# Differential attention on one core: exponentials in their own step, an earlier difference of maps, a gate load on ScalarE's queue

## The chip, the cores and the metric

One core of a Trainium2 chip runs the whole program. The metric is the device time of one execution in microseconds. The engines are TensorE (PE; PEld is its weight load), VectorE (DVE), ScalarE (ACT), GpSimd (POOL) and the queues that issue DMAs, here SyncE's (SPq) and ScalarE's (ACTq).

## The reference

Two layers of a hybrid decoder. Each layer norms its input, projects it to 4224 columns, runs an RWKV-7 branch and a differential attention branch, gates both with SiLU and projects the result back. The prompt has 2048 tokens; 8 decoded sequences of 4 tokens use a paged cache of 2048 past tokens each (16 pages of 128). The change is in the attention alone:

```python
def diff_attend(q, k, v, q_pos, k_pos, lam):
    s = jnp.einsum('bqhcd,bkhcd->bhcqk', q, k) / math.sqrt(DIFF_HEAD_DIM)
    s = jnp.where(k_pos[None, :] <= q_pos[:, None], s, -jnp.inf)
    p = jax.nn.softmax(s, axis=-1)
    attn = p[:, :, 0] - lam * p[:, :, 1]
    return jnp.einsum('bhqk,bkhe->bqhe', attn, v)
...
    o = attend(q, k, v, lam)
    o = rms_norm(o, subln_w, SUBLN_EPS) * (1.0 - lam_init)
    diff_out = o.reshape(B, T, DIFF_WIDTH) * jax.nn.silu(diff_gate.astype(f32))
```

There are 4 heads; each has two maps (c = 0, 1) over 64 dimensions and values of 128.

## The kernel before

A loop over the 2 layers runs five phases, each closed by a barrier: projection, RWKV prompt, attention, RWKV of the decoded sequences, output projection. Every engine has its own program; semaphores order them. Attention is written out flat, with no loop in hardware.

The prompt's attention goes by row tiles of 128 queries: tile t of 64 is head t // 16, step s = t % 16 of that head. `ORDER` alternates short and long rows (0, 15, 1, 14, ...), so that even s have short rows (128 to 1024 keys) and odd s long ones (2048 down to 1152). A row is cut in blocks of 512 keys: `blocks(t)` is 1 or 2 in even steps and 4 or 3 in odd ones. Work on tile t is spread over three steps:

- step t: TensorE makes the scores of both maps per block (`scores`, L1352, and the mask on the last block, L1357) into one of two pairs of PSUM banks; VectorE evicts them to S0 and S1 (`scores_out`, L1259) and then takes the maximum (`maxima`, L1264, L1265), which releases `mx_ok`.
- step t + 1: ScalarE takes the exponentials in place, S0 at j = 0 and S1 at j = 1 (`exp`, L1163), which release `ex_ok`; at the end of the step VectorE forms S0 = S0 + c S1 (`combine`, L1270 to L1272), which releases `cb_ok`.
- step t + 2: TensorE turns the map by blocks through one bank (`turn_map`, L1368), ScalarE copies it out (`copy_turned`, L1172), TensorE multiplies it with the values (`values`, L1380); at the end ScalarE copies the output and its squares (`copy_o`, L1177, L1178), which releases `o_ok`, for which the next tile's values wait.

Step t has `width(t)` = max(blocks(t), blocks(t-2) + 2) places j. From j = 1 on each holds some work beside (`beside`): turning the head's values (L1390, copied at L1210; s = 2 and 3), turning the finished output of the head before (L1397, used at L1295; s = 5 and 7), or the next piece of a decoded sequence: turning a page of keys (L1123, copied by ScalarE at L1039), scores against four pages (L1115, evicted at L1078), the exponentials of all its scores (L1047, L1049, L1050), turning them (L1127, L1132, copied at L1053, L1060), and the products with pages of values (L1143). In each head one sequence has its exponentials around s = 7 and the other one at s = 14. At j ScalarE does the copy of the page that TensorE turns at j + 1.

Once per head VectorE forms sums (`head_sums`, s = 1, L1276 to L1280, needs the last output copy), ScalarE takes their root (`head_root`, s = 4, L1182, with a switch of tables) and VectorE scales the output (`head_scaled`, s = 4, L1287). The gate of the head lies in `cg`: loaded by SP (L1013), its tanh at s = 12 to 15 (L1189), gated at L1291, the head's result formed in place (L1295) and stored by ScalarE's queue at s = 8 of the next head (L1193). The load of the next gate waits for that store.

SP's queue holds the pages of keys (L970; 4 buffers, each waits for its turning) and of values (L979; two groups of 4 pages), the maps' queries and keys (L988), the values (L1008) and the gate, in one order.

Of the kernel before, what the change touches and what calls it, by code (L numbers as in the profile page):

```python
# [45 lines left out]
Q_ROW, K_ROW, V_ROW, DG_ROW = 2176, 2688, 3200, 3712  # L46
# [68 lines left out]
def build(nc, ins, outs):  # L115
# [4 lines left out]
    with ctx:  # L120
# [756 lines left out]
        cg = cv(SEQ)  # L877
# [27 lines left out]
        c_v, c_g, c_lam, c_lv, mask_ok = [csem(n) for n in ("in_v", "in_gate", "lam", "lv", "mask")]  # L905
        c_kq, c_cst, u_in, c_sto = [sem(n) for n in ("c_in_kq", "c_cst", "u_in", "c_store")]
# [74 lines left out]
        def map_rows(l, h, r):  # L981
            return PT[bass.ds(l * COLS + h * P + r, P), 1:SEQ + 1]
# [21 lines left out]
        def attn_sync(sp, l):  # L1004
            def load_values(h):
                if h:
                    t_full(sp, "v", h - 1, 3)
                sp.dma_start(vT[:, :], map_rows(l, h, V_ROW)).then_inc(c_v, 16)  # L1008

            def load_gate(h):  # L1010
                if h:
                    sp.wait_ge(c_sto, 16 * h)
                sp.dma_start(cg[:, :], map_rows(l, h, DG_ROW)).then_inc(c_g, 16)  # L1013
            load_values(0)
            sp.wait_ge(u_in, U_IN)
            keys_sync(sp, l, 0, range(KS))
            for b in range(NSEQ):
                h = b // 2
                keys_sync(sp, l, b, range(KS, 8))
                values_sync(sp, l, b, (0, 1))  # L1020
                if b % 2 and h + 1 < HEADS:
                    load_maps(sp, l, h + 1)
                keys_sync(sp, l, b, range(8, NP))
                if b % 2 and h + 1 < HEADS:
                    load_values(h + 1)
                if b + 1 < NSEQ:
                    keys_sync(sp, l, b + 1, range(KS))
                values_sync(sp, l, b, (2, 3))
                if b % 2 == 0:
                    load_gate(h)  # L1030

        def beside_scalar(act, b, k):
            if K_AT <= k < K_AT + NP:
# [118 lines left out]
        def attn_scalar(act, l):  # L1152
            act.wait_ge(c_lam, 1)
            act.activation(lamv[:, 2:4], lamv[:, 0:2], ACT.Exp).then_inc(c_lam, 1)
            act.wait_ge(u_in, U_IN)
            act.activation(sg_s[:, :, :], g_s[:, :, :], ACT.Tanh, scale=0.5).then_inc(so_rt, 1)

            def exp(t, a):
                i, w = row(t), (row(t) + 1) * P
                if a == 0:  # L1160
                    act.wait_ge(mx_ok, t + 1)
                src = S1[:, t % 2, 0:w] if a else S0[:, t % 3, 0:w]
                e = act.activation(src, src, ACT.Exp, bias=nm[:, t % 2, a:a + 1], accum_out=l12[:, par(t), i, a:a + 1])  # L1163
                if a:
                    e.then_inc(ex_ok, 1)

            def copy_turned(t, j):
                G, w = first(t) + j, min(4, row(t) + 1 - 4 * j)
                act.wait_ge(pt_ok, G + 1)
                if G >= 4:  # L1170
                    act.wait_ge(v_ok, G - 3)
                act.activation(PT_[:, G % 4, 0:w, :], bank[4][:, 0:w * P].rearrange("p (c t) -> p c t", t=P), ACT.Copy).then_inc(pa_ok, 1)  # L1172

            def copy_o(t):
                i = row(t)
                act.wait_ge(v_ok, first(t) + blocks(t))
                act.activation(O[:, par(t), i, :], bank[5][:, 0:P], ACT.Copy)  # L1177
                act.activation(osq[:, :], bank[5][:, 0:P], ACT.Square, accum_out=ssq[:, par(t), i:i + 1]).then_inc(o_ok, 1)  # L1178

            def head_root(h):  # L1180
                act.wait_ge(fs_ok, h + 1)
                act.activation(fs[:, :], fs[:, :], ACT.Sqrt).then_inc(rt_ok, 1)  # L1182

            def gate_tanh(h, g):
                if g == 0:
                    act.wait_ge(c_g, 16 * (h + 1))
                if 4 * h + g >= 2:
                    act.wait_ge(sg_ok, 4 * h + g - 1)
                act.activation(tg[:, g % 2, :], cg[:, g * GRP:(g + 1) * GRP], ACT.Tanh, scale=0.5).then_inc(gt_ok, 1)  # L1189

            def store_head(h):
                act.wait_ge(oe_ok, 4 * h + 4)
                act.dma_start(MT[bass.ds(RW + h * P, P), 0:SEQ], cg[:, :]).then_inc(c_sto, 16)  # L1193
            for t in range(NTILE + 2):
                h, s_ = t // NT, t % NT
                if h and s_ == 8 and t < NTILE:
                    store_head(h - 1)
                for j in range(width(t)):
                    if j < 2 and 1 <= t <= NTILE:
                        exp(t - 1, j)  # L1200
                    if j < blocks(t - 2):
                        copy_turned(t - 2, j)
                    if j == 0 and h and s_ == 4:
                        head_root(h - 1)
                    if j == 0 and 12 <= s_:
                        gate_tanh(h, s_ - 12)
                    if (t, j + 1) in V_AT:
                        vh, vg = V_AT[t, j + 1]
                        t_full(act, "v", vh, vg)
                        act.activation(vtok[:, 4 * vg:4 * vg + 4, :], TB.rearrange("p (c t) -> p c t", c=4), ACT.Copy).then_inc(t_out, 1)  # L1210
                    for b, k in pieces(t, j + 1):
                        beside_scalar(act, b, k)
                if t >= 2:
                    copy_o(t - 2)
            head_root(HEADS - 1)
            act.wait_ge(so_sum, 1)
            act.activation(ors[:, :, :], SB[:, 0:P].rearrange("p (c t) -> p c t", c=4), ACT.Sqrt, bias=lamv[:, 6:7], scale=1.0 / P).then_inc(so_rt, 1)
            store_head(HEADS - 1)
            act.wait_ge(u_lv, 7)
            act.dma_start(MT[RW:D, SEQ:TOK].rearrange("(h p) t -> p h t", p=P), omx[:, :, :]).then_inc(u_sto, 16)  # L1220
            act.wait_ge(u_sto, 16)

        def attn_vector(dve, l):
# [82 lines left out]
            for t in range(NTILE + 2):  # L1306
                h, s_ = t // NT, t % NT
                for j in range(blocks(t)):
                    scores_out(t, j)
                    beside(t, j)  # L1310
                if t < NTILE:
                    maxima(t)
                if 1 <= t <= NTILE:
                    combine(t - 1)
                if 12 <= s_ < 16:
                    gate(h, s_ - 12)
                for j in range(blocks(t), width(t)):
                    beside(t, j)
                if h and s_ == 1:
                    head_sums(h - 1)  # L1320
                if h and s_ == 4:
                    head_scaled(h - 1)
# [763 lines left out]
```

## Time and profile before

| | us |
|---|---|
| median of 3 runs | 4914.3 (4902.1 to 4914.8) |
| profiled execution | 4913.2 |
| its span | 4911.4 |
| TensorE busy | 4096.3 (83%) |
| VectorE busy | 2023.2 (41%) |
| ScalarE busy | 1751.4 (36%) |
| chain that ended last | TensorE 67%, VectorE 12%, ScalarE 8% |
| attention, layer 0 | 1495 to 2177 |
| attention, layer 1 | 3891 to 4578 |

Busy time is that in which an engine executes; TensorE's busy time depends on its granted clock, shown as a share of full speed. A row of the timeline gives start, duration, engine, line, operation, output and inputs with shapes, the number of merged instructions, and in brackets the idle time before it with what ended it. Microseconds are counted from the start of the span. A row of the stretches gives its bounds and length, the busy time and number of instructions of each engine, the mean granted clock, the share of the DMA engines and their rate.

### The profile page before, as it was taken

What the parts mean: (1) busy time and instruction counts of PE and PEld (TensorE: products, weight loads), DVE (VectorE), ACT (ScalarE), POOL (GpSimd) and SP (SyncE); (2) the same over time, 40 slices, a digit from 0 to 9 for tenths busy, and PEclk for the clock granted to TensorE, in tenths of its full rate; (3) what the DMA queues carried; (4) which work ended last, traced back from release to release, by engine and by line L of the source; (5) the groups of instructions that cost most, each with busy time, mean ns of one, the idle gap of its engine ahead of it and who ended that gap; (6) DMA issues with size and microseconds to landing.
All of it is one profiled execution on the core that took longest, in us unless ns stands there. A gap on an engine that the chain in (4) does not pass through costs nothing.

```text
span 4911.4 us, 114297 instructions
## 1 busy us (share of the span) xinstructions
PE 4096.3 (83%) x49138; PEld 3564.4 (73%) x49138; DVE 2023.2 (41%) x4536; ACT 1751.4 (36%) x3584; POOL 481.6 (10%) x264
## 2 busy tenths in 40 slices
PE   3999998788887887877979999978888788788595
PEld 2999998677774555556979999967777555555495
DVE  3111111666655555552231111136666455555335
ACT  3000000666655555651110000036666555565211
POOL 1322231000000000001033222200000000000200
PEclk9999999799998999987989999979999899999697
DMA  4211121111113344343222111111111244353333
GB/s 162 78 70 74 65 77 61 39 44 37 39 45 113 127 147 133 100 146 121 84 75 76 68 74 70 57 63 38 39 44 28 80 143 122 118 164 97 115 120 131
DMA packets 227651, 427.63 MB, mean 87 GB/s; under 512 B 32162, under 2 KB 137636, under 8 KB 212900
## 3 DMA queue, kind: packets, MB, share of 16 engines
q1 hardware_dynamic: 213316, 339.18, 21.7%
q10 hardware_dynamic: 13824, 81.07, 4.1%
q8 instruction: 390, 6.39, 0.5%
q14 instruction: 121, 0.99, 0.1%
HBM read 304.91 MB, written 123.80 MB: 87 GB/s over the span
## 4 chain that ended last, share of the span: by engine, by line
PE 67%; DVE 12%; ACT 8%; issue 5%; SPq 4%; DMA 4%; POOL 1%; ACTq 0%; DVEq 0%
PE psum L1881 10%; PE psum L1882 10%; PE psum L1883 10%; PE psum L1352 4%; PE psum L1380 3%; PE psum L703 3%; PE psum L1526 3%; PE psum L1528 2%; PE psum L1527 2%; PE psum L1368 2%; PE psum L1123 2%; SPq L978 2%; PE psum L700 2%; SPq L979 2%; PE psum L774 1%
## 5 line engine op out<-in xcount | busy, mean ns | idle before, releaser
L1881 PE MATMUL psum<-x_hi,w_parts 128*128 128x416 f32 x2640 | 931.4, 353 | 60.5 <-POOL w_parts L1839 60.5
L1882 PE MATMUL psum<-x_lo,w_parts 128*128 128x416 f32 x2640 | 927.3, 351 | 0.0
L1883 PE MATMUL psum<-x_hi,w_parts 128*128 128x416 f32 x2640 | 926.7, 351 | 0.0
L1848 DVE TENSOR_TENSOR arena<-psum,arena 128x416 f32<-128x416 f32 x330 | 195.5, 592 | 1284.5 <-PE psum L1883 1284.3
L322 ACT ACTIVATE arena<-arena 128x256 f32<-128x256 f32 x16 | 8.2, 514 | 1543.9 <-DVE arena L446 1543.9
L1881 PEld LDWEIGHTS psum<-x_hi,w_parts 128*128 128x128 f32 x2640 | 496.8, 188 | 68.7 <-POOL w_parts L1839 64.2
L1259 DVE TENSOR_SCALAR_CACHE_REDUCE arena<-psum 128x512 f32<-128x512 f32 (+3 forms) x640 | 357.5, 607 | 358.6 <-PE psum L1352 221.9
L1883 PEld LDWEIGHTS psum<-x_hi,w_parts 128*128 128x128 f32 x2640 | 497.1, 188 | 6.5
L1882 PEld LDWEIGHTS psum<-x_lo,w_parts 128*128 128x128 f32 x2640 | 498.2, 189 | 4.4
L1380 PE MATMUL psum<-arena 128*128 128x128 f32 x2176 | 316.9, 288 | 64.0 <-ACT arena L1172 46.8
L1352 PE MATMUL psum<-arena 64*128 64x512 f32 (+3 forms) x1280 | 325.8, 613 | 40.8 <-DVE arena L1259 22.0
L1380 PEld LDWEIGHTS psum<-arena 128*128 128x128 f32 x2176 | 284.1, 202 | 78.3 <-issue 51.4
L1163 ACT ACTIVATE arena<-arena 128x128 f32<-128x128 f32 (+15 forms) x256 | 309.0, 1207 | 8.2 <-DVE arena L1265 8.2
L1705 POOL MEMSET arena<- 128x32 f32 x2 | 0.3, 156 | 2684.0 <-SPq L107 2684.0
L1526 PE MATMUL psum<-m_hi,wo_hi 128*128 128x416 f32 x640 | 229.4, 358 | 39.6 <-DVE m_lo L1497 39.6
L1172 ACT ACTIVATE arena<-psum 128x512 f32<-128x512 f32 (+3 forms) x320 | 170.3, 532 | 248.8 <-PE psum L1368 248.7
L1836 POOL TENSOR_TENSOR w_parts<-arena 128x1024 fp32r<-128x1024 f32 (+1 forms) x68 | 129.0, 1896 | 1305.6 <-PE psum L1883 978.8
L1039 ACT ACTIVATE arena<-psum 128x512 f32<-128x512 f32 x256 | 154.9, 605 | 261.7 <-PE psum L1123 261.6
L1368 PE MATMUL psum<-ident,arena 128*128 128x128 f32 x1088 | 189.6, 292 | 67.7 <-DVE arena L1272 43.7
L1368 PEld LDWEIGHTS psum<-ident,arena 128*128 128x128 f32 x1088 | 124.0, 147 | 162.0 <-DVE arena L1272 68.5
L1528 PE MATMUL psum<-m_hi,wo_lo 128*128 128x416 f32 x640 | 226.5, 354 | 0.0
L703 PE MATMUL psum<-arena 64*64 64x64 f32 x5120 | 196.3, 229 | 35.7 <-DVE arena L508 27.2
(339 smaller groups left out, 6783.8 us busy)
## 6 DMA issues: line engine op xcount, KB each, us to landing
out_proj_t<-arena ACTq DMA_DIRECT2D x66, 1040.5 KB, 4.2
arena<-in_cache_k SPq DMA_DIRECT2D x256, 256.0 KB, 2.8
arena<-in_cache_v SPq DMA_DIRECT2D x256, 256.0 KB, 3.0
arena<-in_w_in SPq DMA_DIRECT2D x66, 512.0 KB, 3.5
arena<-out_proj_t SPq DMA_DIRECT2D x32, 1024.0 KB, 6.7
arena<-out_proj_t SPq DMA_DIRECT2D x96, 257.0 KB, 3.2
m_raw<-mixed_t SPq DMA_DIRECT2D x10, 1664.0 KB, 7.2
x_res<-x_cur SPq DMA_DIRECT2D x10, 1664.0 KB, 18.1
```

The lines of the kernel that those rows point to most:

```text
L703: mm = pe.matmul(b8(2)[at(h, j), ix(c, h), :], Yp[at(h, j), ix(c, h), :], XT[at(h, j), u % 2, ix(c, h), :], start=True, stop=True)
L1163: e = act.activation(src, src, ACT.Exp, bias=nm[:, t % 2, a:a + 1], accum_out=l12[:, par(t), i, a:a + 1])
L1259: x_ = dve.tensor_scalar(dst, bank[2 * (J % 2) + a][:, 0:w], 0.125, NEG, ALU.mult, ALU.max, accum_out=mxp[:, t % 2, a, j:j + 1])
L1352: mm = pe.matmul(bank[2 * (J % 2) + a][:, 0:w], kq[h % 2][hs(a), 0, i * P:(i + 1) * P], kq[h % 2][hs(a), 1, j * GRP:j * GRP + w], start=Tr ...
L1368: mm = pe.transpose(bank[4][:, c * P:(c + 1) * P], S0[:, t % 3, k * P:(k + 1) * P], ident[:, :])
L1380: mm = pe.matmul(bank[5][:, 0:P], PT_[:, G % 4, c, :], vtok[:, k, :], start=(k == 0), stop=(k == i))
L1526: pe.matmul(bank[q % 3][:, 0:TG], wh, mh, start=(k == 0), stop=False)
L1528: mm = pe.matmul(bank[q % 3][:, 0:TG], wl, mh, start=False, stop=(k == KT - 1))
L1848: dve.tensor_tensor(ost[:, b % 2, 1 + g * TG:1 + (g + 1) * TG], bank[q % 8][:, 0:TG], RSTD[:, cols(g)], ALU.mult).then_inc(p_ev, 1)
L1881: pe.matmul(bank[q % 8][:, 0:TG], w_hi[:, b % 3, k, :], x_hi[:, k, cols(g)], start=(k == 0), stop=False)
L1882: pe.matmul(bank[q % 8][:, 0:TG], w_hi[:, b % 3, k, :], x_lo[:, k, cols(g)], start=False, stop=False)
L1883: mm = pe.matmul(bank[q % 8][:, 0:TG], w_lo[:, b % 3, k, :], x_hi[:, k, cols(g)], start=False, stop=(k == KT - 1))
```

## The change

Three edits in the attention phase. The two exponentials of tile t move from step t + 1 (j = 0 and 1, ahead of the copy of a turned map) to the end of step t: in most steps both stand at the last place, behind the page copy there and ahead of `copy_o`. The difference of tile t - 1 moves on VectorE from behind the maximum of step t to behind the first eviction of step t. The gate's load moves from SP's queue, behind the value pages of every second sequence, to ScalarE's queue ahead of s = 10, with the same wait for the store.

```diff
@@ attn_sync
-            def load_gate(h):
-                if h:
-                    sp.wait_ge(c_sto, 16 * h)
-                sp.dma_start(cg[:, :], map_rows(l, h, DG_ROW)).then_inc(c_g, 16)
...
-                if b % 2 == 0:
-                    load_gate(h)
@@ attn_scalar
+            def load_gate(h):
+                if h:
+                    act.wait_ge(c_sto, 16 * h)
+                act.dma_start(cg[:, :], map_rows(l, h, DG_ROW)).then_inc(c_g, 16)
...
+                if s_ == 10 and t < NTILE:
+                    load_gate(h)
                 for j in range(width(t)):
-                    if j < 2 and 1 <= t <= NTILE:
-                        exp(t - 1, j)
                     if j < blocks(t - 2):
                         copy_turned(t - 2, j)
...
                     for b, k in pieces(t, j + 1):
                         beside_scalar(act, b, k)
+                    for a in range(2):
+                        if t < NTILE and j == min(blocks(t) + 1 + a, width(t) - 1):
+                            exp(t, a)
                 if t >= 2:
                     copy_o(t - 2)
@@ attn_vector
                 for j in range(blocks(t)):
                     scores_out(t, j)
+                    if j == 0 and t:
+                        combine(t - 1)
                     beside(t, j)
                 if t < NTILE:
                     maxima(t)
-                if 1 <= t <= NTILE:
+                if t == NTILE:
                     combine(t - 1)
```

## Rows read from the trace of the kernel before

**Rows 1.** Attention stretches: busy PE, PEld, DVE, ACT, POOL; clock, DMA share, GB/s.

```profile
1495.00:2177.00 682.00, 563.04 (x4595) 383.62 (x4596) 370.46 (x1156) 399.78 (x888) 0.00 (x0) 0.92 0.41 129
3891.00:4578.00 687.00, 562.48 (x4606) 385.23 (x4606) 374.72 (x1162) 399.93 (x888) 0.00 (x0) 0.92 0.41 128
```

**Rows 2.** Waits of TensorE in 1495 to 2177: total us, times, longest.

```profile
PE psum L1123 <- DMA arena<-in_cache_k: 25.1, 6, 8.4
PE psum L1380 <- ACT arena L1172: 23.4, 24, 1.9
PE psum L1368 <- DVE arena L1272: 21.0, 12, 3.4
PE psum L1368 <- ACT arena L1172: 12.0, 13, 2.4
PE psum L1352 <- DVE arena L1259: 11.1, 10, 2.3
```

**Rows 3.** Timeline of steps 6 and 7 of head 1: start, duration, and in brackets the wait.

```profile
1722.32 1.80 ACT L1163 ACTIVATE arena<-arena 128x1792 f32<-128x1792 f32 x1
...
1724.74 0.91 PE L1380 MATMUL psum<-arena 128*128 128x128 f32 x6 [1.31 <-ACT arena L1172]
...
1726.88 0.16 DVE L1270 RECIPROCAL arena<-arena 128x1 f32<-128x1 f32 x1 [2.36 <-ACT arena L1163]
...
1729.53 0.66 PE L1368 MATMUL psum<-ident,arena 128*128 128x128 f32 x4 [1.53 <-DVE arena L1272]
...
1731.36 1.66 PE L1352 MATMUL psum<-arena 64*128 64x512 f32 x4 [0.74 <-DVE arena L1259]
```

**Rows 4.** Timeline of steps 4 and 5 of head 1.

```profile
1696.53 1.28 ACT L1182 ACT_TABLE_LOAD   x1
1697.82 0.22 ACT L1182 ACTIVATE arena<-arena 128x16 f32<-128x16 f32 x1
...
1704.64 1.11 PE L1368 MATMUL psum<-ident,arena 128*128 128x128 f32 x4 [3.43 <-DVE arena L1272]
...
1709.17 2.08 PE L1352 MATMUL psum<-arena 64*128 64x512 f32 x4 [1.91 <-DVE arena L1259]
```

**Rows 5.** Timeline of steps 14 and 15 of head 0.

```profile
1639.48 0.69 DVE L1078 TENSOR_SCALAR_CACHE_REDUCE arena<-psum 128x512 f32<-128x512 f32 x1
...
1641.15 1.14 ACT L1047 ACTIVATE arena<-arena 128x1024 f32<-128x1024 f32 x1
...
1641.42 1.55 DVE L1272 SCALAR_TENSOR_TENSOR arena<-arena 128x1280 f32<-128x1280 f32 x1
...
1645.91 0.66 PE L1368 MATMUL psum<-ident,arena 128*128 128x128 f32 x4
```

**Rows 6.** Timeline, TensorE's waits for copies: head 1 s 2, 8, head 0 s 12.

```profile
1676.90 0.47 PE L1380 MATMUL psum<-arena 128*128 128x128 f32 x2 [2.42 <-ACT arena L1210]
...
1744.48 1.13 PE L1380 MATMUL psum<-arena 128*128 128x128 f32 x8 [1.87 <-ACT arena L1172]
...
1624.38 0.71 PE L1380 MATMUL psum<-arena 128*128 128x128 f32 x4 [0.86 <-ACT arena L1172]
```

**Rows 7.** Timelines of SP's queue and of TensorE around step 11 of head 1.

```profile
1757.35 0.33 SPq L1013 DMA_DIRECT2D arena<-out_proj_t  x1
...
1777.08 11.13 SPq L970 DMA_DIRECT2D arena<-in_cache_k  x5
...
1786.01 1.12 PE L1123 MATMUL psum<-ident,arena 128*128 128x128 f32 x4 [8.32 <-DMA arena<-in_cache_k]
```

**Rows 8.** Busy times by stretch, columns as in rows 1.

```profile
1744.00:1750.00 6.00, 5.52 (x52) 3.88 (x52) 2.93 (x7) 4.33 (x11) 0.00 (x0) 0.72 0.01 3
1704.00:1715.00 11.00, 8.06 (x30) 5.42 (x32) 8.39 (x22) 1.79 (x4) 0.00 (x0) 0.53 0.00 0
1768.00:1776.00 8.00, 7.89 (x60) 5.41 (x61) 6.86 (x21) 5.77 (x15) 0.00 (x0) 1.00 0.78 238
1778.00:1786.00 8.00, 0.00 (x0) 0.00 (x0) 0.45 (x2) 0.00 (x0) 0.00 (x0) 0.60 0.92 349
```

## The prediction

> **What bounds the kernel now.** I read the stage table first: the change touches only attention, which runs twice, and in each of the two stretches TensorE is busy 563 us of 682 and of 687 at a mean granted clock of 0.92, while VectorE and ScalarE are busy 370 to 400 us [rows 1]. So TensorE sets the time and 120 us per layer are its idle time; the change can only act on that idle time, and on the clock. The waits of TensorE by releaser come next [rows 2]: in the first layer 25.1 us for a page of keys, 23.4 and 12.0 us for the copy of a turned map (L1172), 21.0 us for the difference of maps (L1272), 11.1 us for an eviction of scores (L1259). The last two are what an earlier difference could take away: 32 us per layer, 64 us in all, is the ceiling. The second layer repeats the first [rows 1], so I work out one and double it.
>
> I name steps within a head s = 0 to 15. Odd steps hold long rows (16 down to 9 blocks of 128 keys), even ones short rows. The timeline of s = 6 and 7 shows the pattern [rows 3]: in s = 6 ScalarE does the first exponential of the long row at 1722.32 (1.80 us), copies a turned map and a page, then does the second; TensorE waits 1.31 us for that copy, VectorE 2.36 us for the second exponential, and TensorE in s = 7 another 1.53 us for the difference and 0.74 us for an eviction queued behind it. So one chain ends last: long exponentials, difference, turning.
>
> **The exponentials, step by step.** Both now stand at the end of their own step, behind the last page copy, so on ScalarE they are back to back; what is queued behind them is the output copy (L1177, L1178), the copy of the next turned map and the next page copy, for which TensorE waits. The first exponential starts only 0.4 us sooner, since the page copy before it is itself paced by TensorE. The order is bought by moving one exponential E in front of the copies.
> - s = 6 and 7: exponentials 1721.9 to 1725.5, output copy and map copy 0.9, so TensorE resumes near 1726.5 instead of 1724.74: +1.75. The difference runs 1726.0 to 1728.5, TensorE reaches the turning at 1729.8 and finds it done: 1.53 gone. The eviction behind it ends at 1730.8, and the scores that began at 1731.36 begin at 1730.9: net -0.5 [rows 3]. All four heads: -2.0 per layer.
> - s = 4 and 5, heads 1 to 3: the square root of a head lies between the two exponentials and switches tables and back, 1.28 us each time (one of the two loads is shown); TensorE then waits 3.43 us for the difference and 1.91 us for an eviction [rows 4]. After the change both exponentials come before the switch: they end at 1697.7 instead of 1701.8, the difference ends at 1700.5, the four scalings behind it at 1704.3, the next eviction at 1705.6, where the scores of 1709.17 can start: -3.5 each, -10.5 per layer. Head 0 has no square root there: +1.9 for E, -2.2 of its waits: -0.3.
> - s = 2 and 3: E is 2.0 (2048 elements, by 1.80 for 1792). The sums of a head on VectorE need the output copy, which now stands behind both exponentials, so VectorE is held until 1678 and the difference ends at 1682.2; scores that began at 1683.10 begin near 1683.9. The wait of 2.42 grows to 4.3, those in s = 3 shrink [rows 6]. +0.8 in heads 1 to 3, +1.0 in head 0: +3.4.
> - s = 8 and 9: E = 1.7 with next to nothing behind it to win back (0 to 0.2): the wait of 1.87 [rows 6] grows to 3.3: +1.4, +5.6 per layer.
> - s = 12 and 13: here TensorE does two blocks of scores before it needs a copy. The pair ends at 1620.4, just when the map is turned, and the second copy no longer stands behind an exponential: the wait of 0.86 [rows 6] goes: -3.4 per layer.
> - s = 10 and 11: +0.9 on TensorE, but in heads 0 to 2 it then waits 8.3 us for a page whose loading is timed by SP's queue [rows 7], which swallows it; head 3 pays. With +1.1 in the last two steps: +2.0 per layer.
>
> **The difference behind the first eviction.** In odd steps it is the short row's and costs nothing: VectorE idles there 2 to 3 us later in the step. In even steps it stands in front of a second eviction, the maximum, and the page work. That hurts at s = 14. There VectorE evicts page scores at 1639.48, on which the page's own exponentials wait (start 1641.15); the difference took 1.55 us plus 0.5 for its two small parts, after them [rows 5]. Moved ahead it pushes the page exponentials to 1642.7. They last 2.6 us (two of 1024 elements at 1.14, and a short one), now followed by both exponentials of a row of 1024 (2.3 us by the same 1.14), the output copy and only then the map copy: done near 1648.4. TensorE, which turned the next map at 1645.91, first waits 1.3 us for the page exponentials and then for that copy: 1648.5 to 1648.7, +2.8 in every head, +11.2 per layer. This is the largest new wait. At s = 0 a similar +1.1 falls into a wait for a page of values that is there already, nothing.
>
> **The gate.** SP's gate issue at 1757.35 leaves its queue, 0.55 us with its register work, between page loads; its wait for the store had long been met (store at s = 8). On ScalarE it is issued at the start of s = 10, near 1767, and takes 0.4 us of its sequencer, beside running activations: 0, at most 0.4 x 8 = 3 us. Its 1 MB now moves beside eight value pages (0.78 of the engines' time, 238 GB/s) and before the two maps and the key page issued at 1777.08, for which TensorE waits until 1786.01; there 349 GB/s flow [rows 7, 8]. If it fits into the spare room, that wait shrinks by 0.55; if it all lands in front, it grows by 1 MB / 349 GB/s = 3.0. I take 0, since s = 10 starts 10 us before that key page is issued.
> The Trainium skill (DMA: Bandwidth & Descriptors, Issuing engines are not separate DMA queues) says that DMAs of any issuing engine run on the same 16 DMA engines and interleave, and that another issuer saves only sequencer time. By that rule the move is worth the 0.55 us at most, and the 3.0 us are a risk; no row of before shows two issuers at once at this place.
>
> **The clock.** Stretches with long waits fall towards the level of 1.2 GHz: 0.53 in 1704 to 1715, 0.60 in 1778 to 1786. Behind the 1.87 us at s = 8 the six microseconds from 1744 had a mean of 0.72: 0.28 x 6 = 1.7 us lost [rows 8]. I charge one such loss more at s = 8 and one at s = 14, 4 x 2 x 1.7 = +13.6 per layer, and give back two thirds of the 0.47 x 11 = 5.2 us in s = 5, 3 x 3.4 = -10: +3.6 per layer.
>
> **Sum.** Per layer -2.0 - 10.5 - 0.3 + 3.4 + 5.6 - 3.4 + 2.0 + 11.2 + 0 = +6.0, with the clock +9.6; two layers +19. The profiled execution took 4913.2 us (span 4911.4), 1.1 below the median 4914.3, so 4932.
> The Trainium skill (ScalarE: Activation LUTs, What ACT_TABLE_LOAD costs) puts a switch at 1283 ns plus a drain of about 1380 ns. The load is that long here, but the square root starts 1.29 us after its load, so the trace shows no drain; by the page, s = 4 would win another 1.38 us for each of the two loads, 16 us over six heads, and the sum would be 4916.
>
> **Rivals.**
> - The early difference pays (4884). The new waits at s = 14, 8 and 2 come out at half (-20 over both layers against my sum) because TensorE has other work there, and the clock terms of +7 turn into -20. For it: 64 us of TensorE's idle time end on VectorE [rows 2]. Against: TensorE's stream is in order and the copies gate it.
> - The new waits throttle (4965). Slower than my forecast: the waits of 3 to 4 us at s = 2, 6, 8 and 14 each bring twice the loss of [rows 8]; it decides from two such waits per head on: 32 places, about 1 us each, +33.
> - The gate load collides (4950): +3.0 in six heads, +18.
> - Waits only change places (4913): what the difference gives, the copies take.
>
> **Chances.** Forecast 0.45 (its own range 4918 to 4950), early difference pays 0.22, throttling 0.13, gate 0.07, no change 0.13. Range 4886 to 4962. A measurement here can tell about 0.3% (15 us), so 4899.6 to 4929.1 is the same: faster 0.20, same 0.28, slower 0.52.
>
> **What would show it.** TensorE's wait for L1272 should fall from 21.0 to under 5 us per layer, that for L1172 rise from 23.4 + 12.0 to over 50, a wait of L1127 for the page exponentials appear, VectorE's wait before L1270 fall at s = 4. I am wrong if the copies' wait stays, or the wait at s = 14 does not appear.

## The result, and the profile after

The kernel with the change takes 4936.7 us (median of 7 runs, 4927.3 to 4944.7) where the one before takes 4912.4 (7 runs on the same chip, 4901.6 to 4914.8): a ratio of 1.0060 [1.0047, 1.0073]: 24.3 us slower by the medians, 29 by the ratio. 4932 was forecast. The profiled execution took 4942.1 us; its page begins:

```profile
span 4940.3 us, 114299 instructions
...
PE 4125.5 (84%) x49138; PEld 3586.3 (73%) x49138; DVE 2019.0 (41%) x4536; ACT 1759.7 (36%) x3584; POOL 481.9 (10%) x264
...
q1 hardware_dynamic: 212164, 330.79, 21.2%
q10 hardware_dynamic: 14976, 89.46, 4.5%
```

The gate's 8.4 MB now go by q10, ScalarE's queue. Only attention grew: from its first to its last TensorE instruction it takes 699.2 and 699.7 us in the two layers, 14.8 more in each. The stretches after the change, columns as in rows 1 (bounds and length, busy PE, PEld, DVE, ACT, POOL, granted clock, DMA share, GB/s):

```profile
1494.00:2194.00 700.00, 581.05 (x4606) 395.39 (x4606) 370.47 (x1160) 404.17 (x888) 0.00 (x0) 0.89 0.40 125
3904.00:4604.00 700.00, 573.23 (x4606) 392.59 (x4606) 370.79 (x1160) 403.71 (x888) 0.00 (x0) 0.90 0.40 125
```

Against [rows 1] this holds a surprise. TensorE's idle time is 700.00 - 581.05 = 119.0 us and 126.8, where it was 119.0 and 124.5. What grew is its busy time, by 15.7 and 10.7 us for the same work, at a clock of 0.89 and 0.90 instead of 0.92. For the first layer of the kernel before, the growth is counted from a row that holds the whole phase: the first stretch of [rows 1] ends at 2177, while the last 11 of the 4606 matmuls run until 2179.4.

```profile
1495.00:2180.00 685.00, 565.44 (x4606) 385.78 (x4606) 373.46 (x1161) 399.78 (x888) 0.00 (x0) 0.92 0.41 128
```

In sum the waits have been exchanged for others, and the same matmuls took longer at a lower clock. Where each of the two happened is worked out by steps further down.

TensorE's waits in 1492 to 2188 (total us, times, longest), to be held against [rows 2]:

```profile
PE psum L1384 <- ACT arena L1166: 35.5, 12, 3.5
PE psum L1372 <- ACT arena L1166: 31.9, 20, 3.6
PE psum L1384 <- ACT arena L1209: 18.0, 4, 4.8
PE psum L1117 <- DMA arena<-in_cache_k: 12.2, 3, 5.1
...
PE psum L1117 <- ACT arena L1033: 7.2, 14, 1.3
PE psum L1121 <- ACT arena L1044: 6.4, 4, 1.6
...
PE psum L1356 <- DVE arena L1261: 1.5, 1, 1.5
```

Lines have moved: L1356 is the scores, L1261 the eviction, L1274 the difference, L1372 the turning, L1166 its copy, L1384 the values, L1209 the copy of the head's turned values, L1117 and L1033 page and copy, L1121 the turning that waits for the page's exponentials (L1044), L1072 the eviction of page scores. The wait for the difference, 21.0 us, is gone from the list, the eviction's fell from 11.1 to 1.5, that for a page of keys from 25.1 to 12.2. In their place, the copy of a turned map rose from 23.4 + 12.0 to 67.4, and a wait of 4 x 1.6 for the page's exponentials is new.

Steps 14 and 15 of head 0, the timeline that answers to [rows 5]:

```profile
1640.58 1.55 DVE L1274 SCALAR_TENSOR_TENSOR arena<-arena 128x1280 f32<-128x1280 f32 x1
...
1643.26 0.69 DVE L1072 TENSOR_SCALAR_CACHE_REDUCE arena<-psum 128x512 f32<-128x512 f32 x1
...
1644.38 1.15 ACT L1041 ACTIVATE arena<-arena 128x1024 f32<-128x1024 f32 x1 [2.41 <-DVE arena L1078]
...
1647.11 0.29 PE L1121 MATMUL psum<-ident,arena 128*32 128x128 f32 x1 [1.60 <-ACT arena L1044]
...
1648.09 1.13 ACT L1157 ACTIVATE arena<-arena 128x1024 f32<-128x1024 f32 x1
...
1649.63 0.58 ACT L1166 ACTIVATE arena<-psum 128x512 f32<-128x512 f32 x1
...
1650.26 1.12 PE L1372 MATMUL psum<-ident,arena 128*128 128x128 f32 x4 [1.80 <-ACT arena L1166]
```

The difference runs ahead of the page's eviction, ScalarE stands idle for 2.41 us, the page's exponentials start late, and both exponentials of the next row follow them before the map is copied: the chain as forecast. TensorE waits twice. Its last row above lasts 1.12 us where the same four matmuls took 0.66 in [rows 5]. The stretch with the two waits and the one behind it:

```profile
1644.85:1650.26 5.41, 2.02 (x17) 1.32 (x15) 2.41 (x8) 5.41 (x15) 0.00 (x0) 0.88 0.00 0
1650.26:1654.00 3.74, 3.74 (x20) 3.41 (x24) 3.64 (x15) 1.71 (x5) 0.00 (x0) 0.50 0.00 0
```

TensorE was busy 2.02 of 5.41 us, and then ran 3.74 us at 0.50 (1.2 GHz): half of them, 1.9 us, are lost, as much as a wait costs. Before the change the clock stood at 1.00 in this place:

```profile
1646.00:1650.00 4.00, 4.00 (x58) 3.63 (x59) 2.89 (x15) 3.46 (x8) 0.00 (x0) 1.00 0.02 4
```

Steps 4 and 5 of head 1, which answer to [rows 4]:

```profile
1706.91 1.28 ACT L1176 ACT_TABLE_LOAD   x1
1708.21 0.21 ACT L1176 ACTIVATE arena<-arena 128x16 f32<-128x16 f32 x1
...
1710.80 1.28 ACT L1157 ACT_TABLE_LOAD   x1
```

Both exponentials of the long row ended at 1706.2, ahead of the first load, and VectorE's wait for them in front of the difference is 2.16 us where it was 5.91. No row of TensorE's timeline between 1710.08 and 1724.34 has a wait; before, it stood 3.43 and 1.91 us there. So a gain at s = 4 and 5 stands against losses at s = 14 and 15, and the experiments take them apart.

### The profile page after: what moved, and what is told of

Read it like the earlier page. It is cut to its first block, busy times and chain, and to the rows that moved or that the text cites. A ratio compares the mean times of both kernels' runs of the same rounds, so it can differ in the third digit from the quotient of the medians.

```text
span 4940.3 us, 114299 instructions
## 1 busy us (share of the span) xinstructions
PE 4125.5 (84%) x49138; PEld 3586.3 (73%) x49138; DVE 2019.0 (41%) x4536; ACT 1759.7 (36%) x3584; POOL 481.9 (10%) x264
## 4 chain that ended last, share of the span: by engine, by line
PE 70%; DVE 10%; ACT 9%; issue 4%; DMA 3%; SPq 2%; POOL 1%; ACTq 0%; DVEq 0%
PE psum L1885 10%; PE psum L1886 10%; PE psum L1887 10%; PE psum L1356 5%; PE psum L1384 4%; PE psum L703 3%; ACT arena L1157 3%; PE psum L1530 3%; PE psum L1532 2%; PE psum L1531 2%; PE psum L1117 2%; PE psum L1372 2%; PE psum L700 2%; PE psum L774 1%; PE psum L1137 1%
## 5 line engine op out<-in xcount | busy, mean ns | idle before, releaser
L1261 DVE TENSOR_SCALAR_CACHE_REDUCE arena<-psum 128x512 f32<-128x512 f32 (+3 forms) x640 | 362.3, 607 | 410.8 <-PE psum L1356 283.5
L1384 PE MATMUL psum<-arena 128*128 128x128 f32 x2176 | 322.1, 293 | 107.0 <-ACT arena L1166 70.9
L1384 PEld LDWEIGHTS psum<-arena 128*128 128x128 f32 x2176 | 290.7, 206 | 116.2 <-ACT arena L1172 103.7
L1356 PE MATMUL psum<-arena 64*128 64x512 f32 (+3 forms) x1280 | 342.4, 641 | 21.8 <-SPq L107 18.7
L1033 ACT ACTIVATE arena<-psum 128x512 f32<-128x512 f32 x256 | 154.5, 604 | 273.5 <-PE psum L1117 273.3
L1372 PE MATMUL psum<-ident,arena 128*128 128x128 f32 x1088 | 186.9, 289 | 64.1 <-ACT arena L1166 64.1
L1372 PEld LDWEIGHTS psum<-ident,arena 128*128 128x128 f32 x1088 | 122.2, 146 | 160.7 <-ACT arena L1166 93.8
L1166 ACT ACTIVATE arena<-psum 128x512 f32<-128x512 f32 (+3 forms) x320 | 170.5, 533 | 187.5 <-PE psum L1372 186.3
L1531 PE MATMUL psum<-m_lo,wo_hi 128*128 128x416 f32 x640 | 225.6, 352 | 0.0
```

Source lines behind the costliest of these rows:

```text
L1261: x_ = dve.tensor_scalar(dst, bank[2 * (J % 2) + a][:, 0:w], 0.125, NEG, ALU.mult, ALU.max, accum_out=mxp[:, t % 2, a, j:j + 1])
L1356: mm = pe.matmul(bank[2 * (J % 2) + a][:, 0:w], kq[h % 2][hs(a), 0, i * P:(i + 1) * P], kq[h % 2][hs(a), 1, j * GRP:j * GRP + w], start=Tr ...
L1372: mm = pe.transpose(bank[4][:, c * P:(c + 1) * P], S0[:, t % 3, k * P:(k + 1) * P], ident[:, :])
L1384: mm = pe.matmul(bank[5][:, 0:P], PT_[:, G % 4, c, :], vtok[:, k, :], start=(k == 0), stop=(k == i))
L1531: pe.matmul(bank[q % 3][:, 0:TG], wh, ml, start=False, stop=False)
```

## The experiments

Theory A, the forecast's: three separate things. The exponentials' move takes the root and its table loads out of the chain to the difference (gain) and delays the copies (loss); the difference's move delays the page's exponentials at s = 14 (loss); the gate's does nothing. Rival B: the early difference pays and the exponentials' delays make the loss. Rival C: the gate's load collides. The ratios are against runs of the kernel before on the same chip, whose medians were 4908.2 us (for the single edits and the late difference at s = 14), 4905.9 (for the two moves of the root and the two edits on top of them) and 4908.6 (for the other three).

**The three edits one at a time.** First the exponentials alone, on the kernel before:

```diff
                 for j in range(width(t)):
-                    if j < 2 and 1 <= t <= NTILE:
-                        exp(t - 1, j)
...
                         beside_scalar(act, b, k)
+                    for a in range(2):
+                        if t < NTILE and j == min(blocks(t) + 1 + a, width(t) - 1):
+                            exp(t, a)
```

> The kernel before with the two exponentials of a tile in its own step and nothing else; the difference stays at the end of VectorE's step, the gate on SP's queue. My theory (the exponentials ahead of the copies cost about one exponential per even step and give back the waits for the difference in s = 5 and 7; the early difference adds only the delay at s = 14): the wait of TensorE for the page exponentials at s = 15 (1.6 us in the changed kernel) is gone, s = 14 and 15 together cost about 2 us over before instead of 4.1, s = 4 and 5 win 5 us in heads 1 to 3, and the time is 8 to 16 us below the changed kernel, +8 to +16 us over before: about 4923. Rival 1 (the early difference is what takes away the waits for the difference): the waits for L1272 stay near 21 us per layer and the time is at or above that of the changed kernel, 4937 or more. Rival 2 (the exponentials alone are the loss and the difference costs nothing): 4937.

Measured: 4914.9 us, 1.0004 [0.9993, 1.0015]. No change that can be told: below the 4923 that was expected and the 4937 of both rivals. The wait for the difference, 21.0 us in twelve places, has fallen to a single one of 1.3 us, at the first tile, without any move of the difference. TensorE's waits of that kernel in the first layer:

```profile
PE psum L1381 <- ACT arena L1172: 35.5, 12, 3.5
PE psum L1369 <- ACT arena L1172: 28.7, 20, 3.6
PE psum L1123 <- DMA arena<-in_cache_k: 22.6, 4, 7.3
...
PE psum L1353 <- DVE arena L1260: 3.2, 5, 1.5
```

Then the difference alone:

```diff
                     scores_out(t, j)
+                    if j == 0 and t:
+                        combine(t - 1)
                     beside(t, j)
                 if t < NTILE:
                     maxima(t)
-                if 1 <= t <= NTILE:
+                if t == NTILE:
                     combine(t - 1)
```

> The kernel before with the difference behind the first eviction and nothing else. VectorE then waits for the second exponential, which is still behind a map copy and a page copy in the next step, in front of the second eviction and the page scores. My theory: at s = 14 the page exponentials start about 3 us later (8 places, +21 us in all), at s = 12 the second eviction comes 1 us too late (+7), the even steps with one block put the maximum behind the difference: +20 to +35 us, about 4940. Rival (VectorE has slack, so the place of the difference is free): 4912, no change.

Measured: 4978.7 us, 1.0128 [1.0106, 1.0150], 63 to 70 us slower by ratio and medians, about twice the upper end of what was expected. VectorE's own waits for the second exponential say why. The kernel before (total us, times, longest):

```profile
DVE arena L1270 <- ACT arena L1163: 89.2, 32, 6.2
```

The kernel after:

```profile
DVE arena L1272 <- ACT arena L1157: 62.0, 32, 8.6
```

The difference alone:

```profile
DVE arena L1270 <- ACT arena L1163: 169.5, 60, 6.3
```

With the exponentials at j = 0 and 1, the second is not done when the first eviction is, and VectorE stands in front of the second eviction. VectorE's timeline of this kernel at step 14 of head 1:

```profile
1822.10 0.17 DVE L1270 RECIPROCAL arena<-arena 128x1 f32<-128x1 f32 x1 [2.57 <-ACT arena L1163]
...
1822.61 1.55 DVE L1272 SCALAR_TENSOR_TENSOR arena<-arena 128x1280 f32<-128x1280 f32 x1
...
1825.30 0.69 DVE L1078 TENSOR_SCALAR_CACHE_REDUCE arena<-psum 128x512 f32<-128x512 f32 x1
```

ScalarE's at the same place:

```profile
1826.41 1.15 ACT L1047 ACTIVATE arena<-arena 128x1024 f32<-128x1024 f32 x1 [3.96 <-DVE arena L1084]
```

ScalarE waits 3.96 us for VectorE in turn. So the two edits are not a sum: alone +2 and +63 to +70, together +24. The own-step exponentials are what makes the early difference bearable. Rival B falls with these two runs: the difference alone does not pay, and the exponentials alone make no loss.

The gate alone:

```diff
-                sp.dma_start(cg[:, :], map_rows(l, h, DG_ROW)).then_inc(c_g, 16)
...
+                act.dma_start(cg[:, :], map_rows(l, h, DG_ROW)).then_inc(c_g, 16)
...
+                if s_ == 10 and t < NTILE:
+                    load_gate(h)
```

> The kernel before with the gate's load on ScalarE's queue ahead of s = 10 and nothing else. My theory: no change, between -5 and +5 us; the page wait at s = 11 moves by less than 1 us. Rival (the 1 MB lands in front of the maps and the key page): that wait grows by up to 3.0 us in six heads, +18 us, 4930.

Measured: 4903.4 us, 0.9985 [0.9971, 0.9998]: at most a small gain, and no loss. Rival C falls.

**The suspected place alone.** The kernel after, with the difference late at s = 14 and nowhere else:

```diff
-                    if j == 0 and t:
+                    if j == 0 and t and s_ != 14:
                         combine(t - 1)
...
-                if t == NTILE:
+                if t == NTILE or s_ == 14:
                     combine(t - 1)
```

> The changed kernel with the difference back behind the maximum at s = 14 alone (4 tiles per layer), early everywhere else. My theory (at s = 14 the early difference delays the page scores' eviction, the page exponentials and with them everything behind on ScalarE): the 1.6 us wait for the page exponentials at s = 15 disappears and the wait for the map copy shrinks from about 1.8 to near 1.5 us, 1.5 to 2.5 us per place, 12 to 20 us in all: about 4921. Rival (the wait at s = 15 comes from the exponentials of the short row standing in front of the copy, whatever VectorE does): same time as the changed kernel, 4937, the wait only changes its name.

Measured: 4908.6 us, 0.9993 [0.9979, 1.0007], 28 us below the change by the medians, 33 by the ratios: this one edit in 8 places, 3.5 to 4.1 us each, takes back a loss as large as that of the whole change. The size was missed (12 to 20 were expected), the mechanism was not: the wait for L1044 is gone from the list, that for L1166 at the turning fell from 31.9 us. TensorE's waits of this kernel in the first layer have:

```profile
PE psum L1372 <- ACT arena L1166: 28.5, 19, 3.6
```

These are 6.4 + 3.4 us of waits in one layer, some 20 in two. In steps 14 and 15 themselves the late difference takes away 24 us over both layers, 15 of them idle time and 9 busy time, which is clock. Summed over attention, its idle time is only 6 us shorter than in the kernel after and its busy time 19 us, mostly because in steps 10 and 11 the kernel after had slower matmuls in place of waiting for a page of keys. So the place itself costs more by its waits than by its clock. With the early difference at all steps but 14 and the gate's edit, this kernel stands at 0.9993 beside 1.0004 for the exponentials alone, so the early difference brings next to nothing on top of them.

The counterpart is a kernel with the exponentials alone in which the row of s = 14 has them where they were:

```diff
+                    if j < 2 and t and (t - 1) % NT == 14:
+                        exp(t - 1, j)
...
-                        if t < NTILE and j == min(blocks(t) + 1 + a, width(t) - 1):
+                        if t < NTILE and s_ != 14 and j == min(blocks(t) + 1 + a, width(t) - 1):
```

> The kernel before with the exponentials in their own step for every tile but that of s = 14, whose two stay at j = 0 and 1 of s = 15 (difference and gate as before). My theory (the 1.5 us left waiting at s = 15 is for the map copy that stands behind the page exponentials and both exponentials of the short row): that wait goes, 1.5 to 2.5 us in eight heads, -12 to -20 us against the run with all exponentials moved, about 4898. Rival (the wait is for the page exponentials alone): no change against that run, 4915.

Measured: 4903.0 us, 0.9986 [0.9973, 0.9999], 9 to 12 us below the exponentials alone, at or under the lower edge of the expected gain; the two intervals overlap by a little. In the profiles, steps 14 and 15 hold 1.1 us less idle time in every head than with all exponentials moved: the pair of exponentials is itself a part of the wait there.

And the difference alone but for s = 12 and 14:

```diff
-                    if j == 0 and t:
+                    if j == 0 and t and s_ not in (12, 14):
...
-                if t == NTILE:
+                if t == NTILE or s_ in (12, 14):
```

> The kernel before with the early difference in every step but s = 12 and 14. In the run with the early difference everywhere, s = 13 took 1.8 us and s = 15 4 to 5 us more than before in each head. My theory (only the even steps with page scores and a second eviction are hurt): 8 x (1.8 + 4.6) = 51 of its 63 us go, about 4922. Rival (every early difference costs, through VectorE waiting in front of evictions): half of it or more stays, 4940.

Measured: 4938.6 us, 1.0045 [1.0031, 1.0058]. Some 40 us of the 63 to 70 lay at s = 12 and 14; 22 to 30 stay, and they lie in the other steps: more than the 12 that my theory left and less than the rival's half or more, so both kinds of place cost. Evictions at which TensorE had waited 10 times and 11.1 us [rows 2] now hold it 21 times, and page scores wait for VectorE, a wait that the kernel before does not have at all in this stretch. TensorE's waits of this kernel in the first layer:

```profile
PE psum L1354 <- DVE arena L1259: 19.6, 21, 1.9
...
PE psum L1115 <- DVE arena L1072: 5.1, 4, 1.3
...
PE psum L1115 <- DVE arena L1078: 3.9, 4, 1.0
```

**Where the gain at s = 4 comes from.** If it is the root and its two loads leaving the chain, then moving the root alone should give it without the delayed copies. First the root behind the second exponential:

```diff
-                    if j == 0 and h and s_ == 4:
+                    if j == 1 and h and s_ == 4:
                         head_root(h - 1)
```

> The kernel before with one line moved: at s = 4 the root of a head (with its two table loads) comes behind the second exponential of the long row instead of between the two. My theory (what the changed kernel wins at s = 4 and 5 is only that the table loads leave the chain from the exponentials to the difference): this one edit gives that gain without the others' losses: the difference ends 2.7 us sooner, TensorE's 3.4 us wait for it at s = 5 falls to about 1.8, and s = 4 and 5 together take about 5 us less in six heads: -30 us, about 4879. Rival (the early start of both exponentials in their own step is what counts): less than -8 us, 4901 or more.

Measured: 4884.2 us, 0.9958 [0.9943, 0.9974], 22 us faster where 30 were expected. TensorE's timeline shows what came and what did not: the wait for the difference has fallen from 3.43 to 1.99, that for the eviction, which stands behind the scalings, is still 1.91.

```profile
1697.92 0.66 PE L1368 MATMUL psum<-ident,arena 128*128 128x128 f32 x4 [1.99 <-DVE arena L1272]
...
1702.44 2.08 PE L1352 MATMUL psum<-arena 64*128 64x512 f32 x4 [1.91 <-DVE arena L1259]
```

Then the root in s = 3, where ScalarE idles, with a one-column exponential behind it that brings the table back there, and the scaling at the end of s = 3:

```diff
-                    if j == 0 and h and s_ == 4:
+                    if j == 2 and h and s_ == 3:
                         head_root(h - 1)
+                        act.activation(dum[:, :], eps_rms[:, :], ACT.Exp)
...
-                if h and s_ == 4:
+                if h and s_ == 3:
                     head_scaled(h - 1)
```

> The kernel before with the root moved into s = 3, where ScalarE idles 3 to 5 us for TensorE, followed by one exponential of a single column that loads the exponential's table back there, and the four scalings of VectorE moved to the end of s = 3 as well. My theory: no table load and no scaling is left in s = 4, so besides the difference the 1.9 us wait for the eviction at s = 5 and the 1.3 us page wait at s = 4 go: -6.5 to -8 us in six heads, -40 to -48 us, about 4865. Rival (the loads or the scalings collide with page copies at s = 3): the gain stays below that of the root behind the second exponential.

Measured: 4871.9 us, 0.9925 [0.9906, 0.9944], 34 us faster, more than the root behind the second exponential brought and less than the 40 to 48 expected: steps 4 and 5 take 6.3 us less in heads 1 to 3, but steps 2 and 3, which now hold the loads, 1.2 us more, 0.8 of it idle time. Both loads are still there, only elsewhere. ScalarE's timeline of head 1:

```profile
1679.69 1.28 ACT L1183 ACT_TABLE_LOAD   x1
1680.99 0.21 ACT L1183 ACTIVATE arena<-arena 128x16 f32<-128x16 f32 x1
1681.22 1.28 ACT L1206 ACT_TABLE_LOAD   x1
```

And TensorE's:

```profile
1693.78 0.66 PE L1370 MATMUL psum<-ident,arena 128*128 128x128 f32 x4 [2.00 <-DVE arena L1274]
...
1695.61 2.08 PE L1354 MATMUL psum<-arena 64*128 64x512 f32 x4 [0.48 <-DVE arena L1261]
```

The wait for the difference is the 2.00 that the first place of the root had already given. New is the eviction's, which has fallen from 1.91 to 0.48.

If the exponentials' move was good only for this, it must cost once the root is out of the way. That kernel with the first edit's exponentials added:

```diff
-                    if j < 2 and 1 <= t <= NTILE:
-                        exp(t - 1, j)
...
+                        if t < NTILE and j == min(blocks(t) + 1 + a, width(t) - 1):
+                            exp(t, a)
```

> The same with the two exponentials in the tile's own step as in the changed kernel (difference at the end of VectorE's step, gate on SP's queue). My theory: once the root is out of s = 4 the exponentials' move has nothing large left to win, and its longer waits for copies at s = 2, 8, 10 and 15 remain: +20 to +35 us over the kernel with the root in s = 3, about 4893. Rival (the own step is a gain by itself, only spoiled elsewhere): at or below the kernel with the root in s = 3.

Measured: 4900.8 us, 0.9986 [0.9973, 0.9999]. 29 us slower than without them, as expected. The same kernel with the moved root and the gate's edit in place of the exponentials':

```diff
-                sp.dma_start(cg[:, :], map_rows(l, h, DG_ROW)).then_inc(c_g, 16)
...
+                act.dma_start(cg[:, :], map_rows(l, h, DG_ROW)).then_inc(c_g, 16)
```

> The kernel with the root in s = 3 and in addition the gate's load on ScalarE's queue ahead of s = 10. My theory: the gate alone measured -0.15% of before (interval -0.29 to -0.02%); the same here: 0 to -14 us against the kernel with the root in s = 3, about 4858, the fastest of all. Rival: the gate's gain was noise, same time as that kernel.

Measured: 4870.7 us, 0.9929 [0.9916, 0.9943], the same as without it. The gate's edit brings nothing that can be told here either.

Last, the exponentials in their own step only where the timeline of the change had shown a gain, the rows of s = 3 and 5, on top of that:

```diff
-                    if j < 2 and 1 <= t <= NTILE:
+                    if j < 2 and 1 <= t <= NTILE and (t - 1) % NT not in (3, 5):
...
+                    if s_ in (3, 5) and t < NTILE and j == width(t) - 1:
+                        exp(t, 0)
+                        exp(t, 1)
```

> The kernel with the root in s = 3 and the gate on ScalarE's queue, and in addition both exponentials in the tile's own step for the tiles of s = 3 and 5 alone (2 of 16). My theory (putting a pair of exponentials ahead of the copies pays only where TensorE waits longer for the difference than for one exponential): steps 4 and 5 take 3 to 4 us less in six heads and 6 and 7 half a microsecond less in eight: -20 to -28 us against the kernel without it, about 4848, 1.2% below before. Rival (in the run with all exponentials moved, the short s = 5 came from the other moves or the clock): less than -6 us, 4865 or more.

Measured: 4865.8 us, 0.9909 [0.9895, 0.9922]: the lowest median of all, 43 us below the kernel before and 71 below the change. But it is only some 5 to 10 us below the one without these two tiles' move, and the intervals of the two overlap; 20 to 28 were expected, and the result is as near to the rival's 4865. What I had left out is that the root's move had already taken most of the waits at s = 5: 2.00 + 0.48 were left there, against which the copy's wait at s = 4 rises from 0.48 to 2.35. TensorE's timeline of this kernel:

```profile
1691.50 0.68 PE L1386 MATMUL psum<-arena 128*128 128x128 f32 x4 [2.35 <-ACT arena L1167]
```

TensorE's waits in 1680 to 1720 show the exchange that the whole change consists of, in one stretch: none for the difference or an eviction is left, and the copy's is 3.1 at its longest.

```profile
PE psum L1386 <- ACT arena L1167: 5.4, 2, 3.1
```

## Why the prediction was right

The sign came out, the place that decides it, and the mechanisms at s = 4 and 14. That the total is only 5 us off is in part luck: waits and clock were both mis-sized, in opposite directions. I measured each pair of steps from the first scores of one step to those two steps later, mean over both layers, against the kernel before:

| us, for one head | forecast, waits | with clock | measured, heads 1 to 3 (head 0) | idle time alone, head 1, layer 0 |
|---|---|---|---|---|
| s = 0, 1 | 0 | 0 | +1.0 (+0.7) | 0.0 |
| s = 2, 3 | +0.8 (+1.0) | same | +1.5 (+1.4) | +1.3 |
| s = 4, 5 | -3.5 (-0.3) | -6.9 (-0.3) | -5.1 (+1.1) | -4.4 |
| s = 6, 7 | -0.5 | same | -0.9 (-1.5) | -0.5 |
| s = 8, 9 | +1.4 | +3.1 | +1.2 (+1.2) | +1.5 |
| s = 10, 11 | 0 (+0.9 in head 3) | same | +0.3 (-0.7) | -3.7 |
| s = 12, 13 | -0.9 | same | -0.1 (-0.7) | -0.1 |
| s = 14, 15 | +2.8 | +4.5 | +4.1 (+4.6) | +2.6 |

Measured, a layer has 6.1 in head 0, 3 x 2.0 in the others, and the rest of its 14.8, 2.7, in the two steps behind the last head (1.1 forecast).

- **s = 14.** The step that carried the forecast. Counted from the step's first scores (1637.56), the page's exponentials start at +6.8 and the turning that waited at +12.7; forecast were +7.0 and +12.8 to +13.0 (1642.7 and 1648.5 to 1648.7, from 1635.74). The late-at-14 kernel shows that this place alone decides the sign.
- **s = 4 and 5.** Right in mechanism: the root moved alone brings 22 and 34 us, and with it gone the exponentials' move costs 29. In size the waits gave 4.0 (3.5 forecast) and the clock only 1.1 of the 3.4 that I gave back. In head 0, without a root, the idle time fell by 0.3 to 0.5, as forecast, and the time rose by 1.1: clock.
- **The longer copies' waits.** Row by row as forecast: the first wait at s = 8 is 3.53 (3.3), that at s = 6 3.07 (1.31 + 1.75), that at s = 2 4.41 (4.3). The clock loss of 1.7 that I charged at s = 8 did not come: the busy time of steps 8 and 9 did not grow. TensorE's timeline of the kernel after at s = 6 and 8:

```profile
1729.53 0.91 PE L1384 MATMUL psum<-arena 128*128 128x128 f32 x6 [3.07 <-ACT arena L1166]
...
1748.61 2.05 PE L1384 MATMUL psum<-arena 128*128 128x128 f32 x8 [3.53 <-ACT arena L1166]
```

- **s = 12, a term that failed.** -0.86 in every head was read from head 0 [rows 6], where the step's scores happened to run slow. The eight matmuls in head 0 and in head 1, TensorE's timeline of the kernel before:

```profile
1616.77 2.96 PE L1352 MATMUL psum<-arena 64*128 64x512 f32 x8
...
1789.61 1.87 PE L1352 MATMUL psum<-arena 64*128 64x512 f32 x8
```

 With a clock of 0.59 in 1616.8 to 1619.7 and 0.93 in 1789.6 to 1791.5, TensorE turned the map 1.1 us earlier in head 1, and there the pair of exponentials (1792.70 to 1795.6 in the kernel after) ends 1.0 us after the turning instead of with it. A new wait of 0.43 and one of 0.34 take what the old one gave. 3.4 us per layer were forecast, some 1 came.
- **"In odd steps it costs nothing"**, said of the early difference, holds in this kernel but not by itself: with the exponentials in the next step it costs 22 to 30 us at steps other than 12 and 14. It is the other edit that pays for it.
- **The gate.** 0 was right. But the load did not move beside the value pages, as I had it: in head 1, issued at 1766.28, it landed at 1771.09, as they began. The rows of the issuing queues after:

```profile
1766.28 0.35 ACTq L1188 DMA_DIRECT2D arena<-out_proj_t  x1
...
1770.86 8.92 SPq L979 DMA_DIRECT2D arena<-in_cache_v  x8
```

 What the Trainium skill (DMA: Bandwidth & Descriptors, Issuing engines are not separate DMA queues) says of another issuer, that it saves sequencer time only, agrees with 0.9985 [0.9971, 0.9998] and with no gain on top of the moved root.
- **What was to be seen.** All four signs came: the difference's wait fell to nothing, the copies' rose from 35.4 to 67.4, the wait for the page's exponentials appeared, and VectorE's at s = 4 fell.
- **Waits and clock, mis-sized both.** The forecast had +6.0 of waits and +3.6 of clock per layer. From the first to the last TensorE instruction of attention, the idle time grew by 3.2 us in both layers together and the time in matmuls by 26.4. The waits grew less because the waits for key pages shrank by 12.9 us in the first layer (25.1 to 12.2), where I had let them swallow only the 0.9 of s = 10. The clock cost more, and elsewhere than I had put it. In heads 1 to 3 the busy time grew by 1.5 us in steps 14 and 15 (1.7 forecast), not at all in steps 8 and 9 (1.7 forecast), and by 1.9 in steps 10 and 11 (nothing forecast). Step 10 of head 1, the kernel before:

```profile
1762.33:1769.16 6.83, 5.54 (x40) 3.93 (x40) 3.58 (x13) 6.10 (x14) 0.00 (x0) 1.00 0.55 163
```

 The kernel after:

```profile
1766.02:1775.01 8.99, 6.51 (x41) 4.88 (x40) 4.58 (x13) 6.21 (x14) 0.00 (x0) 0.83 0.84 270
```

 In heads 0 to 2 this costs next to nothing: step 11 holds the wait for the page, and steps 10 and 11 together take 26.9 us where they took 27.2. So a part of the 26.4 us, some 9, only fills time in which TensorE would have waited. In steps 14 and 15, where the time is lost (34 us over both layers), 21 are idle time and 13 clock.
- **The rivals.** As a sum, the idle time did what "waits only change places" said (3 us more), and TensorE's slowing did more than half of what the rival of throttling added (26.4 where the forecast had 7). Neither came as a whole. The rival's +33 is not what its words give, twice a loss of 1.7 us in 32 places; it is a guess of 1 us for each.
- **The drain.** The sum of 4916 that the Trainium skill's drain (ScalarE: Activation LUTs, What ACT_TABLE_LOAD costs) would have given is off; after the change, too, the root starts 1.30 us after its load began (1706.91 to 1708.21), with no drain to be seen. The switch as a unit to be placed is what paid: 34 us from moving it and its return to where ScalarE idles.

## What to carry to other kernels

Moving work on an in-order engine buys its consumer time at the price of everything that it now stands ahead of: list both sides step by step, and look for the one operation in the chain that nobody needs there (here the root and its table loads, 34 us), which can move without the price. An operation that may have to wait goes behind an engine's short, urgent ones; whether it waits depends on the other edits of the change, so edits on two engines are costed together and not one by one. And before a term is multiplied by the number of heads, its row is looked up in more than one of them, with the granted clock beside it.

## What the runs showed of the hardware that I had not expected

The same idle time does not mean the same time. Attention of the kernel after has 119.0 us of TensorE's idle time in its first layer, as before, and 15.7 us more of busy time for the same work. Step 7 takes 14.0 us in head 1 and 12.4 in head 2 of the kernel before, with 2.3 us idle in each, at a granted clock of 0.88 and 1.00: so single steps are comparable by their idle times, and by their times only over many of them. Step 10 is the clearest case: with the exponentials in their own step it holds 2.5 to 2.7 us of idle time everywhere, and takes 7.96 us at a clock of 1.00 or 8.9 to 9.5 at 0.81 to 0.84. Of its 8 places 6 are slow in the kernel after, 3 with the exponentials alone and 2 with the difference late at s = 14. What settles which of two like steps runs at the lower level was not tried. A change that hardly moves the sum of the waits, 3 us of 240, can still cost 0.6%. But the two sums are not two separate costs: in steps 10 and 11, where TensorE waits for a page of keys in any case, slower matmuls took the place of waiting and cost next to nothing.
